# A decoder block: mixing weights one k-block by 1024 columns, sums in two pairs of banks, and the second tile's steps five slots later

## The reference

```
def token_mixer(h, positions, w_in, ..., w_branch_nsa, w_branch_mla, w_out):
    ...
    merged = gates[:, :, 0] * (o_nsa @ w_branch_nsa) + gates[:, :, 1] * (o_mla @ w_branch_mla)
    return merged @ w_out

def peer_ffn(h, w_q, sub_keys, u, v):
    qry = (h @ w_q).reshape(B, T, PEER_HEADS, 2, half)
    s = jnp.einsum('bthpd,hpnd->bthpn', qry, sub_keys)
    ...
        act = jax.nn.gelu(jnp.einsum('cd,ced->ce', hs, u[es]))
        return jnp.einsum('ce,ced->cd', gs * act, v[es])

x = x + g_a * rms_norm(y, attn_post_g)
```

## Time and profile before

| | |
|---|---|
| median of 3 runs | 2338.18 us (2337.74 to 2341.37) |
| the profiled execution | 2335.3 us, its span 2333.6 us |
| PE busy | 85% of the span, 5203 matmul records |
| DVE, ACT, POOL busy | 50%, 15%, 32% |
| DMA | 828.56 MB, mean 355 GB/s |
| granted TensorE clock | 0.92 on average |

### The profile page before, as it was taken

How to read it: one execution, slowest core, us unless ns; L and a number is a source line. 1 busy time by engine, 2 the same in 40 slices (tenths; PEclk the granted TensorE clock), 3 DMA queues, 4 the chain that set the end, 5 groups by cost and what they waited for, 6 DMA issues and landing times.

```text
span 2333.6 us, 15961 instructions
## 1 busy us (share of the span) xinstructions
PE 1991.9 (85%) x5203; PEld 921.4 (39%) x5203; DVE 1159.1 (50%) x2049; ACT 360.5 (15%) x951; POOL 746.2 (32%) x660
## 2 busy tenths in 40 slices
PE   1789999899989989999888799889787777778777
PEld 0335464444434434455333334334333333333233
DVE  6756224561431327777624525623656555555642
ACT  0001011111221114334200102111111011101100
POOL 2103000010000024556422324423844645464550
PEclk9889889999999988999989999989988898989888
DMA  9978636885879788999999999999999999999995
GB/s 349 367 268 299 241 104 237 314 331 178 289 270 365 245 325 306 421 420 421 417 391 391 408 378 403 418 400 381 422 422 422 421 422 421 422 422 422 421 422 225
DMA packets 188040, 828.56 MB, mean 355 GB/s; under 512 B 16612, under 2 KB 22936, under 8 KB 112196
## 3 DMA queue, kind: packets, MB, share of 16 engines
q0 software_dynamic: 91648, 637.57, 67.2%
q1 hardware_dynamic: 94228, 186.28, 22.6%
q10 hardware_dynamic: 2096, 3.85, 0.4%
HBM read 825.52 MB, written 2.13 MB: 355 GB/s over the span
## 4 chain that ended last, share of the span: by engine, by line
PE 56%; DMA 35%; DVE 5%; issue 2%; POOL 2%; ACT 1%; SPq 0%; DVEq 0%; POOLq 0%; ACTq 0%
DMA arena<-in_peer_v_dram,idx_now 17%; PE PS L1458 12%; PE PS L1040 12%; PE PS L1412 12%; PE PS L1504 12%; DMA arena<-in_ada_w_dram 7%; DMA arena<-in_peer_w_q_dram 4%; DMA arena<-in_w_branch_nsa_dram 4%; DMA arena<-in_w_out_dram 3%; POOL arena L580 2%; DVE arena L1614 2%; DVE arena L1560 2%; PE PS L1209 1%; PE PS L1238 1%; DMA arena<-in_cmp_w_dram 1%
## 5 line engine op out<-in xcount | busy, mean ns | idle before, releaser
L1504 PE MATMUL PS<-arena 128*128 128x512 f32 x1024 | 498.6, 651 | 138.5 <-DMA arena<-in_peer_v_dram,idx_now 138.5
L580 POOL DMA_INDIRECT arena<-in_peer_v_dram,idx_now x256 | 352.4, 1376 | 618.4 <-PE PS L1458 371.0
L1458 PE MATMUL PS<-arena 128*128 128x512 f32 x1024 | 471.6, 606 | 15.9 <-DMA arena<-in_peer_v_dram,idx_now 15.9
L1412 PE MATMUL PS<-arena 128*128 128x512 f32 x768 | 371.4, 629 | 68.9 <-DMA arena<-in_peer_w_q_dram 22.8
L2039 DVE CUSTOM_DVE_ANT_0 arena<-arena 128x2048 f32<-128x2048 f32 x128 | 291.8, 2292 | 243.7 <-DMA arena<-in_peer_u_dram,idx_now 243.5
L1040 PE MATMUL PS<-arena 128*128 128x512 f32 (+1 forms) x912 | 399.1, 591 | 0.2 <-ACT arena L681 0.2
L1504 PEld LDWEIGHTS PS<-arena 128*128 128x128 f32 x1024 | 212.5, 210 | 424.6 <-issue 412.4
L580 POOL DMA_INDIRECT arena<-in_peer_u_dram,idx_now x256 | 313.5, 1225 | 166.4 <-issue 71.3
L2013 DVE CUSTOM_DVE_ANT_0 arena<-arena 128x2048 f32<-128x2048 f32 x128 | 290.9, 2288 | 49.5 <-DMA arena<-in_peer_u_dram,idx_now 46.4
L1458 PEld LDWEIGHTS PS<-arena 128*128 128x128 f32 x1024 | 195.5, 196 | 256.4 <-issue 233.1
L1412 PEld LDWEIGHTS PS<-arena 128*128 128x128 f32 x768 | 148.0, 199 | 259.3 <-issue 184.5
(11 more groups left out here) (247 smaller groups left out, 1159.7 us busy)
## 6 DMA issues: line engine op xcount, KB each, us to landing
arena<-in_ada_w_dram POOLq DMA_DIRECT2D x96, 1024.0 KB, 7.7
arena<-in_w_in_dram SPq DMA_DIRECT2D x112, 512.0 KB, 5.2
arena<-in_w_out_dram SPq DMA_DIRECT2D x64, 512.0 KB, 7.5
arena<-in_peer_w_q_dram SPq DMA_DIRECT2D x64, 512.0 KB, 9.3
arena<-in_w_branch_nsa_dram SPq DMA_DIRECT2D x32, 512.0 KB, 10.6
arena<-in_w_branch_mla_dram SPq DMA_DIRECT2D x32, 512.0 KB, 8.9
arena<-mod_rows SPq DMA_DIRECT2D x7, 1024.0 KB, 19.0
arena<-in_x_dram SPq DMA_DIRECT2D x4, 1024.0 KB, 8.5
```

The lines of the kernel that those rows point to most:

```text
L580: pool.indirect_dma_start(dst, None, tab, bass.IndirectOffsetOnAxis(ap=idx_now[:, now, e:e + 1], axis=0)).then_inc(landed, 16)
L1412: ins = nc.tensor.matmul(PS[:, 4 + j % 3, :], lhs[:, 2 * w + k, :], tile[:, k, :], start=first and k == 0, stop=last and k == 1)
L1458: ins = nc.tensor.matmul(PS[:, k, :], diag[i % 8], Vrow0[i % RING0][:, k * NC:(k + 1) * NC], start=(i == 0), stop=False, skip_group_check= ...
L1504: ins = nc.tensor.matmul(PS[:, 4 + k, :], diag[e % 8], Vrow[e % RING][:, k * NC:(k + 1) * NC], start=(first and e == 0), stop=False, skip_ ...
```

## The change

Three things change. (1) A weight tile of the mixing is one k-block of 128 rows by 1024 columns, so 128 runs of 4 KB, and its two matmuls share the left side and go to two banks. Sums take the pairs of banks 4, 5 and 6, 7 in turn; turns go to banks of the pair that is not being summed, the keys to banks 0 to 3. The order of columns and turns changes with it: 8 tiles to a branch sum of 1024 columns, 16 to a half of the output or the queries; of the first tile, the last four output tiles are gone through bank by bank. Two of the four query slices are done after tile 79, the others after tile 95, and turned and scored at `Q_AT` and `SC_AT`. (2) The second tile's attention and all behind it start at slot 5 instead of 0 (`FIRST1`); `MIX1` goes from 56 to 61. (3) The second tile's mixing takes 2 tiles in a slot throughout. Repeated assignments of `TOPK_AT, GEXP_AT` go away as well.

Of the hunks that are left out, some name the new bank in ACT's and PE's helpers (and let `queries_out` wait for 80 + 16 * (n // 2) tiles), one declares the semaphore `y_part`, and one takes out the repeated lines.

```diff
-        w2ring = at(o_p, W2SLOTS, 2, NC)
+        wide = at(o_w, WSLOTS, 2 * NC)
+        wide2 = at(o_p, W2SLOTS, 2 * NC)
...
-        MERGED_AT, MERGED_LAST, QTR_AT, SC_AT = 3, 4, 2, 5
-        SK_AT = ((1, 3), (1, 6), (2, 1), (2, 4))
-        H2_BANK = (4, 5, 7, 6)
+        TURN_AT, SK_AT = (20, 22, 36, 38), (40, 42, 44, 46)
+        Q_AT, SC_AT = (82, 88, MIX, MIX + 2), (85, 91, MIX + 1, MIX + 3)
+        LAST_OUT = 4
...
-        MIX1 = 2 * UNITS + 8
+        FIRST1 = 5
+        MIX1 = FIRST1 + 2 * UNITS + 8
 
         def unit_slot(n):
-            return 2 * n if n <= NSA_UNITS else 2 * n + 4
+            return FIRST1 + (2 * n if n <= NSA_UNITS else 2 * n + 4)
 
         def head_slot(p, hh):
-            return unit_slot(NSA_UNITS + p) - 2 + hh if p else hh
-
-        NORM = MIX1 + 63 * 4 // 7 + 1
+            return unit_slot(NSA_UNITS + p) - 2 + hh if p else FIRST1 + hh
+
+        NORM = MIX1 + 63 // 2
         H2_SLOT = NORM + 7
 
         def mix_slot(i):
-            return MIX1 + i * 4 // 7 if i < 64 else H2_SLOT + 2 + (i - 64) // 2
+            if i < 64:
+                return MIX1 + i // 2
+            return H2_SLOT + 1 + (i - 64) // 2 if i < MIX else H2_SLOT + 17 + i - MIX
...
-        QTR_SLOT = mix_slot(MIX - 1) + 2
-        SC_SLOT = QTR_SLOT + 1
...
-                stage, n, w = i // 32, i // 8 % 4, i % 8
-                cols = slice(n * NC, (n + 1) * NC)
+                stage, half, k = i // 32, i // 16 % 2, i % 16
+                cols = slice(half * 2 * NC, (half + 1) * 2 * NC)
                 if stage == 0:
-                    return (wn_v if w < 4 else wm_v)[:, 2 * (w % 4):2 * (w % 4) + 2, cols]
-                return (wo_v if stage == 1 else wpq_v)[:, 2 * w:2 * w + 2, cols]
+                    return (wn_v if k < 8 else wm_v)[:, k % 8, cols]
+                return (wo_v if stage == 1 else wpq_v)[:, k, cols]
...
-                load(W_BR + i, mix_src(i))
+                m = W_BR + i
+                sp.wait_ge(w_used, m - WSLOTS + 1)
+                sp.dma_start(wide[:, m % WSLOTS, :], mix_src(i)).then_inc(w_landed[m % WSLOTS], 16)
...
-                sp.dma_start(w2ring[:, i % W2SLOTS, :, :], mix_src(i)).then_inc(w_landed[i % W2SLOTS], 16)
+                sp.dma_start(wide2[:, i % W2SLOTS, :], mix_src(i)).then_inc(w_landed[i % W2SLOTS], 16)
...
-                used(t, 32 + 8 * (n + 1))
+                if t == 0 and n == 2:
+                    act.wait_ge(y_part, 1)
+                else:
+                    used(t, 48 + 16 * (n // 2))
                 if n:
...
+            for c_ in range(4):
                 gates_sigmoid(c_)
-                merged_out(0, c_ - 1)
+            for c_ in range(2):
+                merged_out(0, c_)
             act.wait_ge(eps_ready, 1)
             nc.scalar.activation(msq[:, 15:16], eps[:, :], ACT.Sqrt)
-            merged_out(0, 3)
+            for c_ in range(2, 4):
+                merged_out(0, c_)
+            for b in range(4):
+                keys_out(b)
             for n in range(4):
                 y_square(0, n)
                 gated_square(n)
-                if n < 2:
-                    keys_out(2 * n)
-                    keys_out(2 * n + 1)
...
-                    if s == mix_slot(8 * n + 8 + MERGED_AT if n < 3 else 32 + MERGED_LAST):
+                    if s == mix_slot(TURN_AT[n]):
                         merged_out(1, n)
-                    if s == mix_slot(32 + 8 * n + 7):
+                    if s == mix_slot(47 + 16 * (n // 2)):
                         y_square(1, n)
-                    if s == mix_slot(64 + 8 * n + 7):
+                    if s == (mix_slot(79 + 16 * (n // 2)) if n % 2 == 0 else mix_slot(Q_AT[n - 1])):
                         queries_out(1, n)
-                    if s == (mix_slot(64 + 8 * n + 8 + QTR_AT) if n < 3 else QTR_SLOT):
+                    if s == mix_slot(Q_AT[n]):
                         queries_turned(1, n)
-                    if s == (mix_slot(64 + 8 * n + 8 + SC_AT) if n < 3 else SC_SLOT):
+                    if s == mix_slot(SC_AT[n]):
                         scores_out(1, n)
...
-                if c_:
-                    pe.wait_ge(mtr_out, 4 * t + c_)
                 for k in range(4):
-                    ins = nc.tensor.transpose(PS[:, 7, k * P:(k + 1) * P], merged[t][:, (4 * c_ + k) * P:(4 * c_ + k + 1) * P],
-                                              ident[:, :])
+                    ins = nc.tensor.transpose(PS[:, 6 + c_ % 2, k * P:(k + 1) * P],
+                                              merged[t][:, (4 * c_ + k) * P:(4 * c_ + k + 1) * P], ident[:, :])
...
-                pe.wait_ge(mtr_out, 4)
-                if b:
-                    pe.wait_ge(sk_out, b)
                 for k in range(4):
-                    ins = nc.tensor.transpose(PS[:, 7, k * P:(k + 1) * P], sk_raw[:, 4 * b + k, :], ident[:, :])
+                    ins = nc.tensor.transpose(PS[:, b, k * P:(k + 1) * P], sk_raw[:, 4 * b + k, :], ident[:, :])
...
-                if n:
+                if n % 2:
                     pe.wait_ge(sc_out, 4 * t + n)
-                else:
-                    pe.wait_ge(h2T_ready, 4 * t + 4)
...
-            def bank_free(t, j):
-
-                was = j - 3
-                if 0 <= was < 8:
-                    pe.wait_ge(br_out, 4 * t + was // 2 + 1)
-                elif 8 <= was < 12:
-                    pe.wait_ge(y_sq, 4 * t + was - 7)
-                    pe.wait_ge(y_mul, 4 * t + was - 7)
-                elif was >= 12:
-                    pe.wait_ge(q_nat, 4 * t + was - 11)
-
-            def mix(t, i):
-                stage, n, w = i // 32, i // 8 % 4, i % 8
-                if stage == 0 and n and w == MERGED_AT:
-                    turn_merged(t, n - 1)
-                if stage == 1 and n == 0 and w == MERGED_LAST:
-                    turn_merged(t, 3)
-                if stage == 1 and t == 0 and (n, w) in SK_AT:
-                    turn_keys(SK_AT.index((n, w)))
-                if stage == 2 and n and w == QTR_AT:
-                    turn_queries(t, n - 1)
-                if stage == 2 and n and w == SC_AT:
-                    score_experts(t, n - 1)
-                if stage == 0:
-                    j, lhs, first, last = 2 * n + w // 4, oT[t], w % 4 == 0, w % 4 == 3
-                else:
-                    j, lhs, first, last = 4 + 4 * stage + n, mergedT[t] if stage == 1 else h2T[t], w == 0, w == 7
-                if first:
-                    bank_free(t, j)
-                if stage == 1 and n == 0 and w % 2 == 0:
-                    pe.wait_ge(mtr_out, 4 * t + w // 2 + 1)
-                if stage == 2 and n == 0 and w % 2 == 0:
-                    pe.wait_ge(h2T_ready, 4 * t + w // 2 + 1)
+            def banks_free(t, a):
+
+                if 2 <= a < 6:
+                    pe.wait_ge(br_out, 4 * t + a - 1)
+                if a in (3, 5):
+                    pe.wait_ge(mtr_out, 4 * t + a - 1)
+
+            def tile_of(t, i):
                 if t == 0:
                     tile_ready(W_BR + i)
-                    tile, used = wring[:, (W_BR + i) % WSLOTS, :, :], w_used
+                    return wide[:, (W_BR + i) % WSLOTS, :]
+                pe.wait_ge(w_landed[i % W2SLOTS], w2_landed(i))
+                return wide2[:, i % W2SLOTS, :]
+
+            def mix(t, i):
+                if i in TURN_AT:
+                    turn_merged(t, TURN_AT.index(i))
+                if t == 0 and i in SK_AT:
+                    turn_keys(SK_AT.index(i))
+                if i in Q_AT:
+                    turn_queries(t, Q_AT.index(i))
+                if i in SC_AT:
+                    score_experts(t, SC_AT.index(i))
+                if i >= MIX:
+                    return
+                stage, half, k = i // 32, i // 16 % 2, i % 16
+                if stage == 0:
+                    a, lhs, first, last = i // 8, oT[t], k % 8 == 0, k % 8 == 7
                 else:
-                    pe.wait_ge(w_landed[i % W2SLOTS], w2_landed(i))
-                    tile, used = w2ring[:, i % W2SLOTS, :, :], w2_used
-                for k in range(2):
-                    ins = nc.tensor.matmul(PS[:, 4 + j % 3, :], lhs[:, 2 * w + k, :], tile[:, k, :],
-                                           start=first and k == 0, stop=last and k == 1)
+                    a, lhs, first, last = 2 + i // 16, mergedT[t] if stage == 1 else h2T[t], k == 0, k == 15
+                if first:
+                    banks_free(t, a)
+                if stage == 1 and half == 0 and k % 4 == 0:
+                    pe.wait_ge(mtr_out, 4 * t + k // 4 + 1)
+                if stage == 2 and half == 0 and k in (0, 8):
+                    pe.wait_ge(h2T_ready, 4 * t + k // 4 + 2)
+                used = w2_used if t else w_used
+                if t == 0 and 64 - LAST_OUT <= i < 64:
+                    if i < 63:
+                        return
+                    for b in range(2):
+                        for j in range(64 - LAST_OUT, 64):
```

(63 more changed lines are left out.)

51 lines of the change are left out of this document (14 added, 37 removed).

## The result

The changed kernel takes **2306.74 us** (median of 4 runs, 2303.44 to 2311.86), the kernel before beside it 2337.96 (4 runs, 2334.05 to 2341.37): a ratio of **0.9864**, 95% interval 0.9843 to 0.9886. Forecast were 2311 us, 2295 to 2334. The profiled execution took 2303.44 us, span 2301.7, mean clock 0.93.

The account below looks back on a forecast made before the run. DMA transfers were taken as the bound after about 836 us. 2335.3 - 11 (front) - 5.5 (packets) - 10 (dips) = 2308.8 us profiled, which lay 2.9 us under the median: forecast 2311 us, range 2295 to 2334.

Parts of the forecast that it names:

- The bound: Whole kernel after about 836 us: a fixed number of bytes at 422 GB/s plus losses, by which the change was costed.
- the stretch of 10 us under 300: Sign at the start of the expert rows: no 10 us under 300 GB/s between 855 and 940 us.
- The expert lists come 13.8 us later: First tile: head 0's scores made at tile 85 instead of 77, first expert row issued at 849.8 instead of 836.00 us.
- The tail: First tile's last query tiles: done at 857.2 us, then two slices in series at 5.2 us each, ending at 867.6.
- the hole closes: DMA at 870 to 890 us: with steps five slots later, the eleventh row goes out about 872.5, some 3 us to spare.
- Front, -11 us: Transfers from 830 to 940 us: 4.7 MB more moved by 940, so 11 us less; bounds -15.5 and +5.
- Turn by turn, a third of the bytes: Second tile's mixing: queues alternate packets, so 4 KB runs give weights a third, 140 GB/s, instead of 21%, 86 GB/s.
- the share stays: Rival, second tile's mixing: turns go by whole transfers, so wider runs change only the packet count; 2322 us, chance 0.18.
- The packets' own cost, -5.5: Second tile's mixing weights: half as many packets save 5.5 of 11 us; bounds 0 and -11.
- The dips, -10: Second tile's mixing: a little over half of 18.5 us lost in DMA dips is saved; bounds 0 and -18.5.
- 405 to 412: Sign: GB/s expected over the second tile's mixing, which made 397 in the kernel before.
- PE the bound: Rival, second tile's mixing: small waits lower PE's clock until PE sets the pace; slower, 2355 us, chance 0.11.

Follow-up runs that it names:

- first0: The changed kernel with the second tile's steps starting at slot 0 instead of 5: 2303.70 us.
- lists_early: The changed kernel with second tile's steps from slot 0, first two query slices turned and scored earlier, head 1's scores handed to DVE earlier: 2306.01 us.
- lists_early5: The same as lists_early, but with the second tile's steps left at slot 5: 2298.11 us.
- runs_2k: The changed kernel with the second tile's weights landing in runs of 2 KB, in two areas of the ring: 2321.85 us.
- before_hold: The kernel before, with POOL's first expert row waiting until PE has used 90 of the first tile's 96 mixing weight tiles: 2322.35 us, ratio 0.9931.
- two_queues: The changed kernel with the second tile's weights in 2 KB runs, every second tile from the sixth on issued by ACT through a third queue: 2310.72 us.

## Why the prediction was right, and where not

- **The bound.** Right. The transfers set the time from 850 us on; the losses add up to the change. By the rates, over windows at the same times of two executions whose query tiles start 3.2 us apart: 20 x (424 - 82) / 422 = 16.2, 50 x (421 - 385) / 422 = 4.3 and 498 x (418 - 397) / 422 = 24.8 us, 45.3 in all. Against them stand 840 to 860 us, where the rows now come later: 222 and 182 GB/s in place of 407 and 411, 9.8 us. That leaves 35.5, and the stretch is 35.1 shorter. From 855 to 865 us it is 368 GB/s and from there on over 400, so the stretch of 10 us under 300 that would have spoken against the front isn't there.
- **The expert lists come 13.8 us later.** Right, 13.7: the first row at 50.8 us after the first query tile, forecast 849.8 - 798.93 = 50.9; before 37.1.
- **The tail.** PE's tiles end 57.8 us after the first (forecast 58.3), so the contention with the last weights was read rightly. Two slices in series were taken as 10.4 us; from the copy at 859.92 to the fetch at 867.97 it is 8.05. They do go in series; it is PE that is faster. In the kernel before its turn and scoring of the slice took 1.12 and 2.07 us, at a granted clock of 0.50 (863 to 880 us), here 0.66 and 1.16 for the first slice (clock 1.00) and 0.66 and 1.71 for the second (clock 0.66 in 865 to 868). The prediction had taken over the slow clock's 5.2 us a slice.
- **"With the steps five slots later ... the hole closes."** This step was wrong in its cause. The eleventh row comes early because the scores do, and first0 shows that the five slots add nothing. The prediction had both steps in its chain, and never asked what the first alone would do. PE's first expert row, which the prediction wanted near 879 us, so 80 after the first query tile, comes 74.1 after it, and in first0 81.1 after it: it does come earlier by the slots, and the time doesn't change. The slots count only once DVE is no longer stopped by head 1's scores, as lists_early and lists_early5 show.
- **Front, -11 us (bounds -15.5 and +5).** -12.2 from before to runs_2k, which keeps the second tile's narrow runs, -13.1 in before_hold. By q0's bytes between 830 and 940 us it is 35.38 MB against 31.11: +4.27 MB, 10.1 us, though this execution started its query tiles 3.2 us later.
- **Turn by turn, a third of the bytes.** Right: 759 and 760 packets, 2.79 of 8.31 MB. The rival that the share stays is out. By these counts so is the rule of the Trainium skill (DMA: Bandwidth & Descriptors, Queues, rings and completion order) as it was applied there, a turn of 9 to 17 runs of each queue: runs of 1, 2 and 4 KB took 12, 21 and 34%, one run of each for one row's.
- **The packets' own cost, -5.5 (bounds 0 and -11).** 6.5 to 7.1 us with the one dip of two_queues, about 5 without it. By the Trainium skill (same page, Bandwidth), 3 cycles a packet, the estimate was 2.7.
- **The dips, -10 (bounds 0 and -18.5).** This term was mis-sized: 16.4, and about 18 with that dip, the whole of its bound. I had kept nearly half of the dips for PE's small slack and for the x and modulation rows in SP's queue. With a third of the bytes they cost nothing that the rate shows: 418 GB/s from 1310 to 1330 us, where the row of 8 KB packets passes, and 417 from 1340 to 1360, where the earlier trace rows had 311. The mixing as a whole gave 22.9 where 15.5 were forecast, and 418 GB/s where the prediction named 405 to 412 as its sign.
- **The sum.** 2308.8 for the profiled execution, measured 2303.4; by the stretch -35 in place of -26.5, of which 7.4 are the mixing and 1.2 the front.
- **PE the bound.** Out: the clock in the mixing rose from 0.93 to 0.97, and PE waits for rows and weights there still (25.3 and 24.2 us). One argument against it was misread: the earlier trace rows do not show clock 1.00 wherever PE is busy throughout, as 890 to 940 us has PE busy for all 50 us at 0.94.

## What to carry to other kernels

When two DMA queues are both full, look at their packet counts: if these are equal, as here with runs of 1 to 8 KB, the width of a run sets the share, and a stream that starves beside wide gathers wants wider runs or a second queue. A hole in the transfers may be dug some 35 us earlier, by transfers that started too soon and delayed the chain that asks for the next ones; try holding them back before reordering anything. And where a forecast's chain has two helpers for one effect, price each alone.

## What was not expected of the hardware

- **One packet each in turn, over three queues too.** In 1230 to 1250 us of two_queues 736, 728 and 727 packets, at 8, 2 and 2 KB.
- **A weight packet costs 5 to 7 ns of an engine beside its bytes,** these taken at the 422 GB/s of rows alone. Over 20 us of 16 engines, 320 engine-us: two_queues at 408 GB/s lacks (422 - 408) / 422 x 320 = 10.6 for 1455 packets, 7.3 ns each; runs of 4 KB at 416 to 417 lack 3.8 to 4.5 for 760, 5.0 to 6.0 ns. These are differences of a few GB/s, so the figure is rough.
- **The start of the query tiles scatters by 13 us** (795.32 to 808.51) between executions of kernels that do the same up to there. Most of it is there when the first tile's mixing starts (668.47 to 679.96), so it comes from the part before, and no run here tells why. It is most of the scatter between the executions: the six spans of 2294.0 to 2308.5 us in these profiles are 1498.7 to 1500.0 behind that start.
